# Four places for the split expert blocks, and another order of ScalarE's work in the scatter

## What is computed

```python
def peer_ffn(x, w_q, sub_keys, u_tab, v_tab):          # x: 512 tokens x 1024
    q = (x @ w_q).reshape(B, L, 8, 2, 128)              # 8 heads, two half queries
    s = einsum('blhpd,hpnd->blhpn', q, sub_keys)        # 128 keys for each half
    s_top, i_top = top_k(s, 16)
    cand = s_top[..., 0, :, None] + s_top[..., 1, None, :]
    best, flat = top_k(cand.reshape(..., 256), 16)      # 16 pairs of keys for each head
    expert = i1 * 128 + i2                              # one of 16384 experts
    gate = softmax(best)
    # for each token and each of its 8 x 16 experts e:
    act = gelu(x . u_tab[e])
    y  += act * gate * v_tab[e]
h = layer_norm(2 ** 0.25 * h + y)
```

## Time and profile before

| what | value |
|---|---|
| time, median of 3 runs | 2336.11 us (2335.34 to 2336.6) |
| the profiled execution's own time | 2332.46 us |
| its span, first to last instruction | 2330.6 us |
| TensorE matmul busy | 2219.8 us, 95% of the span |
| VectorE busy | 1596.1 us, 68% |
| GpSimd busy | 1046.1 us, 45% |
| ScalarE busy | 1018.9 us, 44% |
| mean granted TensorE clock | 0.990 |
| DMA, mean over the span | 189 GB/s; up to 398 in a stretch of 41 us of the scatter |

### The profile page before, as it was taken

One profiled execution on the slowest core, in us unless ns is written; L12 is line 12 of the kernel. 1 busy time (PEld: TensorE's weight loads), 2 busy tenths in 40 slices (PEclk: granted clock), 3 DMA queues, 4 the chain that ended last, 5 costly groups with the idle time before them and its releaser, 6 DMA issues. The chain is left out here.

```text
span 2330.6 us, 42892 instructions
## 1 busy us (share of the span) xinstructions
PE 2219.8 (95%) x13978; PEld 1345.9 (58%) x14065; DVE 1596.1 (68%) x3466; ACT 1018.9 (44%) x1807; POOL 1046.1 (45%) x732
## 2 busy tenths in 40 slices
PE   7999999989999999989999999979999999999998
PEld 6455454447888888744645565646666444444443
DVE  6546334016777777624308889989998699998887
ACT  4422324215555455234134344359988344443331
POOL 4522422406555555446036778767765322222220
PEclk9999999999999999999999999999999999999999
DMA  5412312311111111043205889879997999999993
GB/s 202 137 41 68 108 53 72 99 59 31 37 36 36 36 36 36 1 145 127 96 32 174 296 285 303 295 241 352 390 396 253 335 384 390 389 387 355 352 352 143
DMA packets 174424, 440.56 MB, mean 189 GB/s; under 512 B 17424, under 2 KB 83600, under 8 KB 174208
## 3 DMA queue, kind: packets, MB, share of 16 engines
q1 hardware_dynamic: 132864, 288.40, 36.1%
q0 software_dynamic: 36864, 134.23, 16.0%
q10 hardware_dynamic: 4608, 16.78, 1.8%
HBM read 395.31 MB, written 44.04 MB: 189 GB/s over the span
## 5 line engine op out<-in xcount | busy, mean ns | idle before, releaser
L2254 POOL TENSOR_TENSOR hid_u_lo<-hid_u,hid_u_hi 128x1024 bf16<-128x1024 f32 x128 | 291.0, 2274 | 166.7 <-ACT hid_u_hi L2238 160.5
L153 PE MATMUL bank<-hT_hi,hid_u_hi 128*128 128x384 bf16 x1024 | 335.1, 327 | 18.3 <-POOL hid_u_lo L2254 7.4
L217 POOL TENSOR_TENSOR w_shared_lo<-w_raw,w_shared_hi 128x1024 bf16<-128x1024 f32 x72 | 155.1, 2176 | 400.4 <-ACT w_shared_hi L212 335.1
L153 PE MATMUL bank<-hT_hi,hid_u_lo 128*128 128x384 bf16 x1024 | 334.8, 327 | 0.0
L153 PE MATMUL bank<-hT_lo,hid_u_hi 128*128 128x384 bf16 x1024 | 334.8, 327 | 0.0
L2238 ACT ACTIVATE hid_u_hi<-hid_u 128x1024 bf16<-128x1024 f32 x128 | 134.9, 1055 | 211.3 <-PE bank L153 201.3
L153 PE MATMUL bank<-hT_hi,w_shared_hi 128*128 128x264 bf16 (+4 forms) x683 | 192.3, 289 | 13.3 <-ACT dn_conv_out L1567 10.5
L153 PE MATMUL bank<-hT_lo,w_shared_hi 128*128 128x264 bf16 (+4 forms) x686 | 193.2, 290 | 1.4 <-ACT ex_grid L2432 1.2
L153 PE MATMUL bank<-hT_hi,w_shared_lo 128*128 128x264 bf16 (+4 forms) x686 | 193.1, 289 | 0.1
L153 PEld LDWEIGHTS bank<-hT_hi,hid_u_hi 128*128 128x128 bf16 x1024 | 100.4, 98 | 88.7 <-issue 23.4
L2945 PE MATMUL bank<-w_shared_lo,ex_gated_hi 128*128 128x512 bf16 x384 | 146.5, 382 | 5.1 <-DVE ex_gated_lo L3027 4.3
(11 more groups left out here) (531 smaller groups left out, 5600.6 us busy)
## 6 DMA issues: line engine op xcount, KB each, us to landing
hid_u<-in_peer_u SPq DMA_DIRECT2D x128, 512.0 KB, 4.8
ex_v<-in_peer_v SPq DMA_DIRECT2D x128, 512.0 KB, 7.5
w_raw<-in_w_ret SPq DMA_DIRECT2D x60, 512.0 KB, 4.4
expert_hidden<-hid_gelu SPq DMA_DIRECT2D x128, 192.0 KB, 4.1
ex_gated<-expert_hidden SPq DMA_DIRECT2D x128, 192.0 KB, 5.2
w_raw<-in_w_dn SPq DMA_DIRECT2D x32, 512.0 KB, 4.0
expert_weights<-ex_grid ACTq DMA_DIRECT2D x32, 512.0 KB, 6.6
ex_weights<-expert_weights SPq DMA_DIRECT2D x64, 256.0 KB, 6.1
```

What stands on the lines that cost most here:

```text
L153: last = nc.tensor.matmul(out, left[l], right[r], start=start and i == 0, stop=stop and i == len(PASSES) - 1)
L217: self.nc.gpsimd.tensor_tensor(self.pairs[slot][1][:, m % 4, :, :], self.raw[:, m % self.RING, :, :], self.pairs[slot][0][:, m % 4, :, :], ...
L2254: self.nc.gpsimd.tensor_tensor(self.us[1][:, m % 2, :, :], self.u32[:, m % RING, :, :], self.us[0][:, m % 2, :, :], ALU.subtract).then_inc ...
```

## The change

The split halves get four places instead of two; ScalarE's order in the scatter is turned, so that the split of block n+2 comes behind the grid copies and the low one-hots of step n; SP's two operations of a step change places. What makes room for the larger halves: several small tiles of the retrieval (`chosen`, `rank_half`, `ranks`) and the scatter's `keys_of` are laid into `incoming.gated`, which is unused until the end of the scatter, and the products of the row dots that nobody reads go to two unused rows of `w_raw`.

```diff
+SPLITS = 4
...
-        self.us = [sbuf(nc, ctx, f"hid_u_{n}", [P, 2, KC, P], BF16) for n in ("hi", "lo")]
+        self.us = [sbuf(nc, ctx, f"hid_u_{n}", [P, SPLITS, KC, P], BF16) for n in ("hi", "lo")]
...
     def split_hi(self, act, n, m):
         act.wait_ge(self.u_in[m % RING], (16 // RING) * (n - m % RING) + 16)
-        if m >= 2:
-            act.wait_ge(self.formed, n - 1)
-        self.nc.scalar.activation(self.us[0][:, m % 2, :, :], self.u32[:, m % RING, :, :],
+        if m >= SPLITS:
+            act.wait_ge(self.formed, n - (SPLITS - 1))
+        self.nc.scalar.activation(self.us[0][:, m % SPLITS, :, :], self.u32[:, m % RING, :, :],
                                   ACT.Copy).then_inc(self.u_hi, 1)
...
     def split_lo(self, pool, n, m):
         pool.wait_ge(self.u_hi, n + 1)
-        if m >= 2:
-            pool.wait_ge(self.formed, n - 1)
+        if m >= SPLITS:
+            pool.wait_ge(self.formed, n - (SPLITS - 1))
...
-        self.spent = [incoming.gated[:, :, :].rearrange("p a n -> p (a n)")[:, 0:D],
-                      incoming.weights[:, :, :, :, :].rearrange("p a s k t -> p (a s k t)")[:, 0:D]]
+        self.spent = [spare[:, RING - 2 + i, :] for i in range(2)]
...
-                def store_and_load(n, m):
+                def load_and_store(n, m):
+                    hidden.load(sp, n + RING, m + RING)
                     hidden.store(sp, n, m)
-                    hidden.load(sp, n + RING, m + RING)
...
-        keys_of = sbuf(nc, ctx, "spread_keys_of", [P, 2, DENSE, ALIKE], BF16)
+        keys_of = incoming.gated[:, :, :].rearrange("p a n -> p (a n)").bitcast(BF16).rearrange(
+            "p (k t a) -> p k t a", k=2, a=ALIKE)
...
                 def step(n, m, side, turn, in_span, u0):
-                    hidden.split_hi(act, n + 2, m + 2)
                     hidden.apply_gelu(act, n, m)
...
                     ahead = turn + (u0 + per) // SLOTS
-                    if isinstance(ahead, int) and ahead == DENSE // TURN:
-                        return
-                    low_halves(ahead, (u0 + per) % SLOTS,
+                    if not isinstance(ahead, int) or ahead < DENSE // TURN:
+                        low_halves(ahead, (u0 + per) % SLOTS,
...
+                    hidden.split_hi(act, n + 2, m + 2)
```

33 lines of the change are left out of this document (17 added, 16 removed).

## The result

The changed kernel takes 2388.23 us (median of 4 runs, 2386.0 to 2389.9), the kernel before in the same comparison 2335.73 us (4 runs, 2334.0 to 2336.6). The ratio is 1.022, with an interval of 1.0207 to 1.0233: 52.5 us slower, where the forecast said 19.8 slower and a range up to 2371. The direction was right, the size was not, and the time lies outside the range.

The account below looks back on a forecast made before the run. TensorE, busy 95% of the span, was taken as the bound, with a ring of dependences binding the changed scatter. 32.3 us lost there minus 12.5 gained in the retrieval, on 2336.1, gave 2355.9 us; range 2345 to 2371.

Parts of the forecast that it names:

- The ring (part 2): Scatter: the turned order closes a two-block ring of dependences, 11.49 us or 5.75 us a block; the scatter loses 32.3 us.
- Start of the ring: Scatter's start: the ring starts with block 78, beginning at 1566.3 us, its last matmul starting at 1570.05.
- The ring is the bound, and each of them gets idle time.: Scatter: TensorE's 4.79, ScalarE's 4.6 and VectorE's at most 4.95 us a block are all below 5.75.
- Rival 3: Scatter: VectorE or the loads join the ring, a round has 12.4 us, loss 53, time 2377 us; chance 0.07.
- Rival 4: Scatter: TensorE's clock falls; with one block in four low, 46 us more (3.8 a block), 2402 us; chance 0.04.
- Part 1: Retrieval: four places bring split and low half about one block earlier, removing TensorE's standing time; gain 12.5 us, bounds 10 to 14.2.
- room for 2.5 us in a tile: Retrieval: VectorE's choice of the last tile precedes TensorE's use by 2.5 us; 10 us in four tiles, the gain's lower bound.
- SP's new order costs nothing: SP's queue: the load waits for a block TensorE has already begun, so it doesn't hold the store; cost nothing.
- so they come earlier too: Retrieval: gathers stand behind GpSimd's low halves and come earlier; 1.28 us of VectorE's time there is waiting for a gathered row.
- The sum: Whole kernel: 32.3 lost minus 12.5 gained is 19.8 us on 2336.1, giving 2355.9 us, 0.85% slower.

Follow-up runs that it names:

- experiment 4: Changed kernel with GpSimd issuing six gathers instead of four ahead of the scatter's first step, turned order kept; 2353.17 us.
- Experiment 2: Kernel before with only ScalarE's turned order in the scatter, two places, SP storing before it loads; 2386.37 us.
- experiment 5: Changed kernel with the split of block n+2 between the grid copies and the low one-hots; 2337.22 us.
- Experiment 7: Changed kernel with ScalarE's old order and two gathers instead of four issued ahead of the scatter's first step; 2370.00 us.
- experiment 1: Changed kernel with ScalarE's old order in the scatter, four places and SP's new order kept; 2338.16 us.
- experiment 3: Changed kernel with split and low half made three blocks ahead in the scatter instead of two, ScalarE's order still turned; 2370.12 us.
- experiment 6: Changed kernel with the split three blocks ahead and six gathers instead of four ahead of the scatter's first step; 2336.32 us.
- experiment 11: Changed kernel with ScalarE's old order, seven eighths of each low half left out from block 78 on; 2319.57 us.
- experiment 8: Kernel before with four places alone, SP storing before it loads and ScalarE's old order; 2337.55 us.
- experiment 12: Changed kernel with ScalarE's old order and each low half made by two GpSimd instructions of half the columns; 2323.03 us.

## Why the prediction was right or wrong

- **The ring (part 2).** Right. 11.2 to 11.4 us a round in the changed kernel's first rounds and 11.35 on average in experiment 4 (261.1 / 23), for 11.49; most of the difference is the low half, 2.13 us instead of 2.24. Experiment 2 shows that places have no part in it, experiment 5 that the eight low one-hots are the link that decides.
- **Start of the ring.** Close, partly by luck (experiment 2: 351.6 us for 352.5, two errors of opposite sign). With four places it is off: from block 75 to block 78 the sum has 30.3 us, the changed kernel 24.6, because VectorE's choice comes earlier and its first one-hot starts 7.7 us after E of block 75 instead of 11.1.
- **"The ring is the bound, and each of them gets idle time."** This is the step that failed, and it cost 29.9 us. The working of part 2 follows one queue past which the split was moved, ScalarE's, and stops at GpSimd's low half. Behind that low half stand GpSimd's next gathers. VectorE's dots then stood 7.9 us behind their gather's issue instead of 10.3, and there was almost no room: in the kernel before, VectorE already waited for rows 7 times, for 3.3 us. A round was not 11.49 us but 12.8 (294.2 / 23). Experiment 7 has the price of late rows alone (35 us in the stretch, 32 in the median), experiment 4 the gain from earlier ones (33 us in the stretch, 35 in the median). That the rows also took longer to land from about 1600 us on made it worse; the working had no term for either.
- **Rival 3** had the place right (loads join the ring) and was dismissed with a sum of busy times: VectorE needs 9.9 us in a round of 11.5, so it gets ahead. But VectorE gets no further ahead than the rows are. Its round of 12.4 us was near the measured 12.8, by another cause than the one it names.
- **Rival 4**, the clock, was taken as an alternative and was a consequence. As long as the ring alone stops TensorE, for about 1 us in a block, the clock is 1.00 (experiment 4); once late rows made the standstills longer, seven blocks ran partly at the lower level. Their longer matmuls are 13.4 of the 29.9 us; the other 16.5 us are waiting. The price of 3.8 us for a block in one of four was too high: the excess was 1.5 to 2.9 us. The Trainium skill ("TensorE: Matmul & The Clock Gate", section "A second HAM failure mode: psum-queue depth-cycling") says that frequent short idle times between groups of matmuls can make the clock swing between its levels. Here the frequent ones, of 1.6 us at most in experiment 4, did not; the clock fell in the kernels with standstills like those at block 88.
- **Part 1, the gain of 12.5 us.** The mechanism was right, the size depends on something that the step left out. All 14.3 us of standstills in the tiles went, and the change of stage gained another 3 us. But "room for 2.5 us in a tile" took VectorE's operations at the lengths they had while GpSimd was often waiting; with GpSimd running on, they got longer, and two changes of tile took back 13.4 us. The changed kernel gave 0.9 us in the retrieval, and 3.7 up to block 78; the same code in experiments 1, 3 to 7 and 11 gave 4.3 to 9.6 in the retrieval and 8.0 to 11.4 up to block 78.
- **"SP's new order costs nothing."** Right as a cost, incomplete as an account: in experiment 8 the places without it removed 6.2 of the 14.3 us of standstills.
- **The gathers, "so they come earlier too".** That held for the retrieval, where VectorE's waits for rows, 10.4 us before, went to nothing; in the scatter the opposite was true.
- **The sum.** Experiment 4, the changed kernel with rows in time, has 2353.2 us for a forecast of 2355.9. That closeness is partly luck: up to block 78 it gained 6.9 us in the retrieval instead of 12.5 and lost 5.6 us less than summed on the way to block 78, which cancel. The ring itself, 261.1 us for a forecast of 264.3, was no luck.

## What to carry to other kernels

When an instruction moves back in one queue, follow it through every queue that waits for it, and list what is queued behind the waiter there, DMA issues above all: a transfer issued one step later needs as much room at its landing, and the room is read from how its consumer waits today. An engine that is below its bound by busy time is no evidence that its work comes in time. Where VectorE's operations with two SBUF operands run beside GpSimd's, take their lengths from when both are busy, and try cutting the GpSimd instruction in two: here it gave 0.7% on the kernel of experiment 1, which has a buffer that takes up the later end, and cost 0.4% on the kernel before, which has none.

## What the runs showed of the hardware

- VectorE's product with two SBUF operands lasts 0.42 us alone and 2.35 us when it starts 0.07 us behind GpSimd's subtraction of 2.13 us; the dot with one operand in PSUM keeps 1.21 us (experiment 1).
- An addition of 0.41 us stood for 4.56 us beside four GpSimd subtractions in a row (experiment 12), and one of 128x1024 as long beside two (changed kernel): VectorE did not get in between them. In the scatter of experiment 12 a product got in between two and was done after 1.37 us.
- Two kernels with the same work on VectorE differ by 9 to 13 us over 46 blocks (234.9 and 238.6 us against 247.2 and 247.7). VectorE's two one-hots and product of a slot took 1858 ns in the one and 2029 in the other, with GpSimd's low halves falling elsewhere among them.
- In the kernel before, gathered rows landed 5.1 to 6.6 us after their issue at 1559 to 1596 us, and up to 9.1 us after it in the next 20 us, while the DMA rate of 41 us stretches went from 293 to 398 GB/s.
- TensorE's granted clock stayed at 1.00 over 200 us with standstills of about 1 us in each block (experiment 4, the longest 1.6), and went to 0.93 where some were as long as those at block 88 (changed kernel: 1.28 and 2.64 us with 0.62 us of matmuls between; experiment 7: up to 4.3). After a wait at a change of tile, 30 score matmuls took 5.31 us, where 32 took 3.74 before.
